# Difference attention of a two-block transformer kernel: the filler's pace, the identity products' slots and the first mean's wait

## The reference

```python
def diff_attention(q, k, v, lam):          # per block of 128 queries, causal
    s = jnp.einsum('bqhcd,bshcd->bhcqs', qb, k) * d ** -0.5      # c = 2 maps of 64 dims
    p = jax.nn.softmax(jnp.where(causal, s, -jnp.inf), axis=-1)
    a = p[:, :, 0] - lam * p[:, :, 1]
    return jnp.einsum('bhqs,bshe->bqhe', a, v)                   # v has 128 dims a head

def odd_mixer(h, ...):
    q, k, v = jnp.split(h @ w_in, 3, axis=-1)     # rope on q and k
    o = diff_attention(q, k, v, lam)
    o = rms_norm(o, subln_g) * (1.0 - lambda_init)               # over the 128 dims of a head
    return o.reshape(b, s, DIFF_W) @ w_out
```

## Time and profile before

| | |
|---|---|
| median of the runs | 2559.94 us |
| the profiled execution | 2559.96 us |
| its span | 2558.3 us |
| TensorE busy | 2501.0 us (98%) |
| VectorE busy | 1532.8 us (60%) |
| ScalarE busy | 1053.4 us (41%) |
| the stage of the change, slots 0 to 34 | 1965.34 to 2119.20 us |

### The profile page before, as it was taken

One profiled execution on the slowest core, in us unless ns is written; L12 is line 12 of the kernel. 1 busy time (PEld: TensorE's weight loads), 2 busy tenths in 40 slices (PEclk: granted clock), 3 DMA queues, 4 the chain that ended last, 5 costly groups with the idle time before them and its releaser, 6 DMA issues.

```text
span 2558.3 us, 31124 instructions
## 1 busy us (share of the span) xinstructions
PE 2501.0 (98%) x12413; PEld 1964.0 (77%) x12413; DVE 1532.8 (60%) x2299; ACT 1053.4 (41%) x1629; POOL 76.6 (3%) x154
## 2 busy tenths in 40 slices
PE   8999999999998999999999999999999999999999
PEld 6667877778866877777777578888878767788887
DVE  6996788686555487867667653333364775533334
ACT  5354333334555342323644743222254763522223
POOL 2000000000000001000000000000000000000000
PEclk9999999999999999999999999999999999999999
DMA  6123366553222256554321023323223113233321
GB/s 177 51 82 99 119 193 183 162 170 95 79 79 77 72 161 208 161 166 143 84 91 57 1 66 116 95 87 99 82 66 99 50 34 84 84 98 99 95 79 58
DMA packets 328095, 262.46 MB, mean 103 GB/s; under 512 B 13658, under 2 KB 312862, under 8 KB 327952
## 3 DMA queue, kind: packets, MB, share of 16 engines
q1 hardware_dynamic: 312256, 206.13, 27.3%
q0 software_dynamic: 15696, 54.34, 6.6%
HBM read 258.32 MB, written 2.12 MB: 102 GB/s over the span
## 4 chain that ended last, share of the span: by engine, by line
PE 88%; DVE 4%; ACT 4%; DVEq 1%; issue 1%; SPq 0%; DMA 0%; ACTq 0%; PEldq 0%; PEld 0%
PE ps L430 59%; PE ps L444 6%; PE ps L448 6%; PE ps L452 6%; PE ps L1481 2%; PE ps L2105 1%; PE ps L2633 1%; PE ps L1495 1%; PE ps L1519 1%; ACT tmpB L1589 1%; ACT probsT L1570 1%; DVE wL L396 1%; ACT wH L369 1%; ACT tmpA L698 1%; DVE tmpB L1640 0%
## 5 line engine op out<-in xcount | busy, mean ns | idle before, releaser
L396 DVE TENSOR_TENSOR wL<-raw,wH 128x2048 fp32r<-128x2048 f32 (+1 forms) x184 | 413.0, 2245 | 125.1 <-ACT wH L369 119.3
L369 ACT ACTIVATE wH<-raw 128x2048 fp32r<-128x2048 f32 (+1 forms) x184 | 343.7, 1869 | 238.3 <-PE ps L430 100.0
L430 PE MATMUL ps<-hH,wH 128*128 128x512 f32 x1656 | 427.7, 400 | 0.1
L430 PE MATMUL ps<-hH,wL 128*128 128x512 f32 x1656 | 425.2, 399 | 0.0
L430 PE MATMUL ps<-hL,wH 128*128 128x512 f32 x1656 | 424.8, 398 | 0.0
L430 PEld LDWEIGHTS ps<-hH,wH 128*128 128x128 f32 x1656 | 307.8, 188 | 85.1 <-issue 13.7
L430 PEld LDWEIGHTS ps<-hH,wL 128*128 128x128 f32 x1656 | 309.2, 188 | 82.9 <-issue 10.8
L430 PEld LDWEIGHTS ps<-hL,wH 128*128 128x128 f32 x1656 | 309.4, 188 | 76.8 <-issue 4.5
L1066 DVE TENSOR_TENSOR tmpB<-ps,tmpB 128x512 f32<-128x512 f32 x44 | 30.4, 691 | 228.2 <-PE ps L430 228.2
L1003 ACT ACTIVATE tmpA<-ff_up,cols 128x512 f32<-128x512 f32 x88 | 67.0, 809 | 238.2 <-DVEq L1030 238.2
L444 PE MATMUL ps<-gH,wH 128*128 128x512 f32 x480 | 155.0, 399 | 2.5 <-issue 1.0
(11 more groups left out here) (407 smaller groups left out, 3283.3 us busy)
## 6 DMA issues: line engine op xcount, KB each, us to landing
raw<-w_up SPq DMA_DIRECT2D x132, 512.0 KB, 5.3
mod_ring<-w_mod POOLq DMA_DIRECT2D x96, 512.0 KB, 4.3
raw<-w_down SPq DMA_DIRECT2D x32, 1024.0 KB, 5.9
raw<-w_gate SPq DMA_DIRECT2D x44, 512.0 KB, 4.0
raw<-w_down SPq DMA_DIRECT2D x16, 768.0 KB, 4.4
raw<-w_in_even SPq DMA_DIRECT2D x9, 1024.0 KB, 5.1
raw<-w_out SPq DMA_DIRECT2D x8, 1024.0 KB, 5.2
raw<-w_in_odd SPq DMA_DIRECT2D x16, 512.0 KB, 5.0
```

What stands on the lines that cost most here:

```text
L369: last = act.activation(wH[:, st.part, 0:st.size], raw[:, st.slot, 0:st.size], ACT.Copy)
L396: last = dve.tensor_tensor(wL[:, st.part, 0:st.size], raw[:, st.slot, 0:st.size], wH[:, st.part, 0:st.size].bitcast(F32), ALU.subtract)
L430: last = pe.matmul(dst, left, right, start=(t == 0 and k == 0), stop=(t == 2 and k == self.kt - 1))
```

## The change

`pace` goes from 24 to 26, so that the 36 filler steps fill slots 0 to 25: 2, 1, 2, 1, 1, 2, 1, 2, 1, 1, 2, 1, 1, 2, 1, 2, 1, 1, 2, 1, 2, 1, 1, 2, 1, 1. The 12 tiles end in slots 1, 3, 5, 7, 10, 12, 14, 16, 18, 20, 23 and 25. The slots with identity products go from 26 to 31 (3 and 2 each) and 32 (8) to 29 to 31 and 32. `mean` waits for bank 0 alone, which is the bank that it writes; the last filler tile lies in bank 1 and is read in slot 27.

```diff
             def mean(self, pe, batch):
                 if batch == 0:
-                    for signal, count in self.free:
-                        pe.wait_ge(signal.sem, count)
+                    signal, count = self.free[0]
+                    pe.wait_ge(signal.sem, count)
                 heads = self.heads[batch]
...
-        mixed = Mixed([dif_pair(p) for p in range(8)], (3, 5), (rest,), pace=24, values_ready=dif_values_ready, norm=HeadNorm(), busy={**{s: (3, 2) for s in range(26, 32)}, 32: (0, 8)}, busy_bank=1,
+        mixed = Mixed([dif_pair(p) for p in range(8)], (3, 5), (rest,), pace=26, values_ready=dif_values_ready, norm=HeadNorm(), busy={**{s: (3, 2) for s in range(29, 32)}, 32: (0, 8)}, busy_bank=1,
                       outs=[2, OUT_BANK] * 4, first_use={2: [(bank_read[2], bank_read[2].count)]}, last_split=(35, 35))
```

## The result

The changed kernel is slower. Its median is 2569.68 us (7 runs, 2564.61 to 2572.88), the kernel before has 2562.1 us beside it (7 runs, 2558.97 to 2564.64): ratio 1.0037, 95% interval 1.0028 to 1.0046. The forecast was 2565.0 us with 2561.4 to 2568.0 as range, so the direction of the likeliest case was right (1.0037 also lies above its line of 0.2%, to which it gave 0.39), the size was too small, and the median lies above the range. The profiled execution is the fastest of the seven, 2564.61 us.

What follows compares the result with a forecast made beforehand. TensorE, busy 98% of the span, was taken as the bound, with ScalarE's ordered queue a second chain. Base 2559.96 us, plus 3.4 for the order and 1.6 for a clock fall, gave 2565.0 us, range 2561.4 to 2568.

Steps and rivals of the forecast that it cites:

- the likeliest case: Whole kernel: later order plus one fall of the clock, 2565.0 us; chance 0.42.
- its line of 0.2%: Whole kernel: a change under 5.1 us can't be told, above 2565.06 us counts as slower; chance of slower 0.39.
- The order: Slots 0 to 28 and on: ScalarE's queue makes TensorE wait, +3.4 us in all, slot 24 beginning 3.2 later.
- L(23): Start of slot 23's logits: 10.2 us after slot 21's, with TensorE idle 3.3 us.
- the line that was named: Source lines to end waits: ScalarE's L1570 before slot 23's logits, VectorE's L709 before slot 28's, about 2.5 us.
- By heads the shift: Slots 4 to 23, five heads: start times shift by +0.6, -0.1, +1.0, -0.8 and +2.6 us.
- Slots 24 to 28 and the end: Slots 24 to 28 last 15.95 us for 15.84, +0.1; removing 15 identity products and bank 1's wait gives nothing.
- L(28) - L(27): From slot 27's logits to slot 28's: 4.5 us against 3.84, set by the last rope behind VectorE's maxima.
- The clock: Stage: one fall to half clock for 3.5 us, costing 1.6 us.
- The sum: Whole kernel: 2559.96 + 3.4 for the order + 1.6 for the clock = 2565.0 us.
- one of two holes: Where the clock may fall: 3.3 us idle before slot 23's logits, or idle of 2.5 and 1.1 in slots 27 and 28.
- The rival of two falls or of one twice as long: Clock falls in both holes or lasts double: +3.4 + 3.3 to 4.5, so 2567 to 2568 us; chance 0.16.

Runs made afterwards that it cites:

- experiment 5: Changed kernel with identity products in every hole its trace shows (slots 7, 10, 15, 19, 23, 26, 28): 2564.4 us, ratio 1.0014.
- Experiment 4: Changed kernel with filler steps at 1, 2, 2, 1 per head to slot 21, then 2, 1, 1, 0, 1, identity products in slots 26 and 28: 2557.72 us.
- experiment 3: Changed kernel with pace back at 24, so only the later identity products and the mean's wait for bank 0 alone remain: 2561.6 us, ratio 1.0004.
- experiment 7: Changed kernel with steps at 1, 2, 2, 1 to slot 21, then 2, 1, 1, 0, 1, without identity products in slots 26 and 28: 2558.71 us, ratio 0.9990.
- experiment 2: Changed kernel with identity products put into the holes of slots 23, 26 and 28 only: 2567.43 us, ratio 1.0023.
- experiment 8: Against Experiment 4, one step moved from slot 18 to 19 and one from slot 20 to 24: 2556.37 us, ratio 0.9984.
- experiment 1: Changed kernel again, no edit, for its spread and a second trace: 2569.04 us, ratio 1.0029.
- the two looks: Two more profiled executions of the changed kernel, no edit: 2568.48 and 2568.32 us.
- the second look: The later of two further profiled executions of the unedited changed kernel: 2568.32 us.

## Why the prediction was wrong

**The order: right in mechanism, a little small.** It said that two steps fewer in slots 0 to 23 save nothing, because ScalarE's copy stands behind its swaps and strip part, and that slot 24 opens 3.2 us later. The trace confirms place by place: waits before the logits of slots 10 (1.86 us for 1.9), 15 and 19 (1.49 and 1.48 for 1.3), 23 (3.36 for 3.3, with L(23) at 10.47 after L(21) for 10.2) and 28 (2.40 for 2.5), each ended by the line that was named. At full clock (experiment 5) slot 24 opens 3.7 us later for 3.2 forecast, and the stage is 3.9 us longer for 3.4. By heads the shift is +0.5, -0.2, +1.2, -0.5 and +2.7 us, so what is missing lies in slots 12 to 19, where two waits were put 0.2 us too short. Experiment 4 is the proof that it is ScalarE's list: other places for the same steps, ending in the same slot, take 7.2 us off the stage (150.54 against 157.73, both at full clock).

**Slots 24 to 28 and the end: right at full clock.** L(28) - L(27) is 4.6 us for 4.5, and from slot 24 to the end of the stage experiment 5 is 0.1 us longer than before, as forecast; removing the identity products and the bank's wait changed nothing that could be told in the median (experiment 3). In the traces the products held the clock up. All five traces in which the 2.4 us hole before slot 28 is left open have a fall behind it (four of the changed kernel and experiment 7), and none of the four with products there has one (experiments 2, 4, 5 and 8); in experiment 3 the clock falls at slot 26 instead. What that is worth, 0.8 and 1.2 us of the stage there, is too little to be told in the medians.

**The clock: the step that failed.** The sum took one fall of the clock for 1.6 us, and placed it in one of two holes. The number of falls, their length and the price by place are wrong. In the stage the four traces of the changed kernel have 6.8, 10.2, 10.2 and 13.7 us at half clock, in two or three of the holes of slots 10, 23 and 28, and their stages last 159.42, 160.69, 160.80 and 162.47 us: 1.7, 3.0, 3.1 and 4.7 more than the 157.73 of the same order at full clock, 3.1 on average. By the medians the clock costs 3.7 us (7.6 apart for the changed kernel, 3.9 with the holes filled), by the ratios 0.15 to 0.23%, 4 to 6 us. The price was right in one place only. Behind slot 22 a fall of 3.4 us costs 1.5 us (slot 23 takes 7.30 us for 5.76), near the 1.7 forecast, but one of 6.8 us costs 2.9. Behind slot 28, where the forecast had some 1.5, one of 3.4 us costs 0.2 (slots 28 to 30 together take 12.49 us in the first trace for 12.30 in experiment 5) and one of 6.8 us costs 1.4 (13.67 us in experiment 1). The holes before slots 10, 15 and 19, of 1.5 to 1.9 us, were in the sum as waits and were left out as places where the clock could fall. The rival of two falls or of one twice as long had 0.16 and ended at 2568. Two falls or more is what every trace shows. That the first execution, 2564.61 us, agrees with the forecast is luck: it has two falls that cost 1.7 us together, where the forecast had one for 1.6, and it is the fastest of seven.

**The base.** The prediction set its sum on 2559.94 us, the median of three. In the comparisons behind it the kernel before has 2562.1, 2561.42 and 2560.5 us. So 2.2 of the 4.7 us between forecast and median are the base of that comparison. The other 2.5 are the 7.6 us between the medians less the 5.0 forecast: 0.5 for the order and some 2 for the clock. As a ratio the forecast was 1.0020, and 1.0037 was measured.

**What stays open.** The four traces make the changed stage 7.0 us longer on average. The medians are 7.6 us apart in both comparisons, but the ratios say 9.5 and 7.4 us, and why the first ratio lies so far from its medians the record does not show. The seven first executions have mean granted clocks of 0.998 for the fastest, 0.995 and 0.996 for three of 2567.9 to 2569.7 us and 0.993 to 0.995 for the three of 2572.5 to 2572.9 us. So the slower executions have the lower clock, and the two at 0.993 lie below every traced one (0.995 to 0.998); whether it is low in this stage or elsewhere is not known, since neither was traced. No fall at slots 15 or 19 was seen in a trace.

## What to carry to other kernels

A filler that is spread evenly over slots is not placed: when its by-products (copies, splits) hang on an engine with its own fixed order, ask in which slot each of them falls and what that engine owes the critical one behind it. Here the same 36 steps over the same 26 slots, with nothing else changed, gave 0.9990 (experiment 7) or 1.0037. A hole in TensorE's work has a second price beside its length, paid in the matmuls behind it, and that price differs by execution and by what runs there: count the holes like the 1.9 us of slot 10 too, not only the longest, and give the range its high side. Identity products in a hole are worth what the fall costs there: 1.5 to 3 us a time behind slot 22, 0.2 to 1.4 behind slot 28. When a hole moves, look whether they should move with it.

## What the runs showed of the hardware

- In the stage of these traces the granted clock stayed at 1.2 GHz for 3.4 or 6.8 us at a time, and a fall can come in the hole or when TensorE is at work again: in the first trace of the changed kernel the hole before slot 23 ends at 2074.29 and the clock is low from about 2075.1.
- The longer falls are those that came earlier against the hole. Before slot 23 the fall came 0.7 and 0.4 us ahead of the hole's end in the two looks and lasted 6.8 us; it came 0.3 and 0.8 us behind it in the other two traces and lasted 3.4 us. Before slot 28 it came 0.3 and 0.7 us behind the end of the 2.4 us hole and lasted 6.8 us (experiments 7 and 1), and 1.3 to 2.1 us behind it and lasted 3.4 us (the first trace and the looks). Nine falls show this; no run varied it by itself.
- The same hole of 1.9 us before slot 10 brought the clock down in two of five traces that have it unfilled (experiment 2 and the second look).
- The price of such a stretch depends on what it meets: 1.5 to 1.6 us of 3.4 in slots 10 and 23, where TensorE is the bound, and behind slot 28, where it waits for ScalarE anyway, 0.2 us of 3.4 (the first trace) and 1.2 of 6.8 (experiment 7).
